# Eight norms of a two-block kernel: sums of squares with tokens on partitions, and one product that spreads the inverse

## The reference

```python
def layer_norm(x, g, b):                      # ln_in, and ln1 and ln2 of both layers
    mu = mean(x, -1); var = mean((x - mu)**2, -1)
    return (x - mu) * rsqrt(var + 1e-5) * g + b

def rms_norm(x, g):                           # before the mixer, before the experts, at the end
    return x * rsqrt(mean(x * x, -1) + eps) * g

x = layer_norm(x, ln_in)
for l in range(2):
    x = layer_norm(ALPHA * x + mixers(x), ln1[l])
    x = layer_norm(ALPHA * x + ffn(x), ln2[l])
x = x + g1 * mixer(modulate(rms_norm(x, norm1), ...))
x = x + g2 * experts(modulate(rms_norm(x, norm2), ...))
return rms_norm(x, final_norm)
```

## Time and profile before

| what | value |
|---|---|
| median of 3 executions | 3438.56 us (3436.9 to 3443.4) |
| profiled execution, its own time | 3444.45 us |
| span of its instructions | 3442.6 us |
| mean granted TensorE clock (of 1.00) | 0.976 |
| PE busy | 3278.4 us (95%) |
| DVE busy | 2461.8 us (72%) |
| ACT busy | 1684.0 us (49%) |

### The profile page before, as it was taken

One profiled execution on the slowest core, in us unless ns is written; L12 is line 12 of the kernel. 1 busy time (PEld: TensorE's weight loads), 2 busy tenths in 40 slices (PEclk: granted clock), 3 DMA queues, 4 the chain that ended last, 5 costly groups with the idle time before them and its releaser, 6 DMA issues.

```text
span 3442.6 us, 43580 instructions
## 1 busy us (share of the span) xinstructions
PE 3278.4 (95%) x13510; PEld 2317.1 (67%) x13510; DVE 2461.8 (72%) x2995; ACT 1684.0 (49%) x2237; POOL 484.7 (14%) x625
## 2 busy tenths in 40 slices
PE   8989999999988999979999999799999999999997
PEld 3453677774453777756646657688878887878885
DVE  4874655454954746554548984799999999999996
ACT  3332433232341423232221133588888888878884
POOL 0000000000000000000000000233434433343340
PEclk9989999999989999999999999899999999999999
DMA  5111334331101443321110022699999999999995
GB/s 199 61 31 43 115 118 135 117 92 61 50 25 49 132 138 116 117 98 43 50 61 13 25 80 86 213 354 367 371 354 358 373 372 351 366 365 357 361 375 194
DMA packets 168015, 618.37 MB, mean 180 GB/s; under 512 B 18528, under 2 KB 18656, under 8 KB 167328
## 3 DMA queue, kind: packets, MB, share of 16 engines
q1 hardware_dynamic: 157232, 573.90, 46.3%
q0 software_dynamic: 10672, 43.00, 4.4%
HBM read 587.99 MB, written 28.84 MB: 179 GB/s over the span
## 4 chain that ended last, share of the span: by engine, by line
PE 79%; DVE 13%; issue 3%; ACT 2%; DMA 2%; POOL 0%; DVEq 0%; ACTq 0%; POOLq 0%; SPq 0%
PE bank L605 52%; PE bank L1241 24%; DVE w_part L2665 2%; DMA sb_ring<-in_w 2%; DVE sb_work L1925 1%; DVE sb_rstd L1887 1%; PE bank L1231 1%; PE bank L1192 1%; PE bank L1249 1%; DVE sb_work L2073 0%; DVE sb_work L2431 0%; DVE sb_work L2387 0%; DVE sb_work L2698 0%; ACT w_part L1790 0%; DVE sb_work L2693 0%
## 5 line engine op out<-in xcount | busy, mean ns | idle before, releaser
L2665 DVE TENSOR_TENSOR w_part<-sb_ring,w_part 128x1024 fp32r<-128x1024 f32 x762 | 889.8, 1225 | 65.0 <-ACT w_part L1790 64.3
L1790 ACT ACTIVATE w_part<-sb_ring 128x1024 fp32r<-128x1024 f32 x762 | 770.0, 1053 | 82.4 <-PE bank L1241 53.8
L1241 PE MATMUL bank<-w_part,xg_hi 128*128 128x512 f32 x2048 | 564.0, 397 | 0.0
L605 PE MATMUL bank<-h_hi,split_part 128*128 128x512 f32 x1408 | 444.4, 400 | 7.9 <-ACT h_hi L1521 7.9
L1241 PEld LDWEIGHTS bank<-w_part,xg_hi 128*128 128x128 f32 x2048 | 383.0, 188 | 89.1
L1241 PE MATMUL bank<-w_part,xg_lo 128*128 128x512 f32 x1024 | 321.0, 395 | 0.0
L605 PEld LDWEIGHTS bank<-h_hi,split_part 128*128 128x128 f32 x1408 | 265.7, 190 | 80.4 <-issue 15.6
L1241 PE MATMUL bank<-w_part,act_hi 128*128 128x512 f32 x1024 | 284.9, 400 | 2.0 <-DVE act_lo L2708 0.9
L605 PE MATMUL bank<-sb_hT,sb_ring 128*128 128x512 f32 x576 | 261.6, 612 | 11.7 <-ACT sb_hT L1342 11.7
L605 PE MATMUL bank<-h_lo,split_part 128*128 128x512 f32 x704 | 272.3, 394 | 0.0
L605 PE MATMUL bank<-act_hi_ff,split_part 128*128 128x512 f32 x704 | 229.1, 407 | 5.7 <-DVE act_lo_ff L2246 5.7
(11 more groups left out here) (364 smaller groups left out, 4728.5 us busy)
## 6 DMA issues: line engine op xcount, KB each, us to landing
sb_ring<-in_w SPq DMA_DIRECT2D x768, 512.0 KB, 7.9
sb_ring<-in_wstream SPq DMA_DIRECT2D x304, 512.0 KB, 3.6
y_rows<-sb_padc POOLq DMA_DIRECT2D x1, 4096.0 KB, 17.7
sb_xT<-in_x SPq DMA_DIRECT2D x4, 512.0 KB, 7.2
x_rows<-sb_padc SPq DMA_DIRECT2D x1, 2048.0 KB, 9.8
residual<-sb_hT POOLq DMA_DIRECT2D x1, 2048.0 KB, 6.5
sb_hT<-residual POOLq DMA_DIRECT2D x1, 2048.0 KB, 8.1
x_rows<-sb_work SPq DMA_DIRECT2D x1, 2048.0 KB, 6.6
```

The source lines that it names most:

```text
L605: ins = nc.tensor.matmul(out, l, r, start=start, stop=stop)
L1241: ins = nc.tensor.matmul(out[n][:], l[:, k, :], r[:, n * 512:(n + 1) * 512], start=False, stop=(k, p) == (KD - 1, 2))
L1790: nc.scalar.activation(w_hi[t % SPLITS], ring[:, t % RING, :], ACT.Copy).then_inc(s_hi, 1)
L2665: nc.vector.tensor_tensor(w_lo[t % SPLITS], ring[:, t % RING, :], w_hi[t % SPLITS].bitcast(F32), ALU.subtract).then_inc(s_lo, 1)
```

## The change

Eight norms (`BY_TOKEN`, and ln1 and ln2 in both layers) get another way to their inverse. The tile `dev_tok` is new: 128 partitions x 2 slots x 8 columns.

- Sums: for each chunk k, and each of the four blocks b of 128 tokens, the 128x128 block of squares is now the stationary operand and two columns of `ones_d` are the moving one. 32 products of two columns take the place of 8 products of 512 columns. Tokens come out on partitions: 8 columns, two equal ones for each block.
- Root: on 8 columns, into `dev_tok`. Reciprocal: on the same 8 columns.
- New on VectorE: a multiplication of the identity (128x128, for all four blocks) by the inverse, broadcast along the free dimension, into `rstd`: four diagonal blocks side by side, 128x512.
- New on TensorE: one product of the 128x128 of ones with these 512 columns (`spread_inverse`), into a PSUM bank of its own. All partitions of it hold the inverse of all tokens.
- The scaling by gain and inverse reads the inverse from that bank.
- In `ln1` the modulation piece stands between the sums and the product that spreads.

```diff
+                if tag[0] in BY_TOKEN:
+                    state["var"] = bank("var", tag)
+                    for k in range(n):
+                        token_var(tag, k)
+                else:
+                    chunks(("var", tag), lambda k: ones, lambda k: squares(width)[:, at + k, :], n, width=width,
+                           ready=("square", tag))
                 if ("var", tag) in MOD_AT_SPOT:
                     modulation(MOD_AT_SPOT["var", tag])
+                if tag[0] in BY_TOKEN:
+                    spread_inverse(tag)
+
+            def token_var(tag, k):
+
+                pe.wait_ge(*reached("square", tag, k))
+                for b in range(TB):
+                    mm(state["var"][:, 2 * b:2 * b + 2], sq[:, k, b * P:(b + 1) * P], ones_d[:, 0:2], (k, b) == (0, 0), (k, b) == (KD - 1, TB - 1),
+                       *(("var", tag) if (k, b) == (KD - 1, TB - 1) else ()))
+
+            def spread_inverse(tag):
+
+                out = bank("inv", tag)
+                pe.wait_ge(dve_done, when("diag", tag))
+                mm(out[:], const("ones"), rstd[:, when("diag_slot", tag), :], True, True, "inv", tag)
...
+            state["var"] = bank("var", ("x1",))
             for k in range(KD):
-                running("var", ("x1",), sq, k, ("square", ("x1",)))
+                token_var(("x1",), k)
+            spread_inverse(("x1",))
...
                     if half == 1 and i in (4, 6, 8, 10):
-                        out2_var((i - 4) // 2)
+                        token_var(("x2",), (i - 4) // 2)
...
             for m in range(4, KD):
-                out2_var(m)
+                token_var(("x2",), m)
             state["job"] = 1
+            spread_inverse(("x2",))
...
                 if m >= 2:
-                    running("var", ("final",), sq, m - 2, ("square", ("final",)))
+                    token_var(("final",), m - 2)
...
+            spread_inverse(("final",))
...
+                if tag[0] in BY_TOKEN:
+                    slot = len(norms) % 2
+                    norms.append(tag)
+                    found[("diag_slot", tag)] = ("slot", slot)
+                    dev = dev_tok[:, slot, :]
+                    dve.wait_ge(act_done, when("deviation", tag))
+                    nc.vector.reciprocal(dev, dev).then_inc(dve_done, did.up())
+                    dve.wait_ge(dve_done, did.n)
+                    nc.vector.tensor_tensor(rstd[:, slot, :].rearrange("p (b t) -> p b t", t=P),
+                        const("ident").unsqueeze(1).to_broadcast([P, TB, P]), dev.rearrange("p (b n) -> p b n",
+                        n=2)[:, :, 0:1].to_broadcast([P, TB, P]), ALU.mult).then_inc(dve_done, did.up(("diag", tag)))
+                    dve.wait_ge(pe_done, when("full", "inv", tag))
+                    return bank_of("inv", tag)[:]
...
+BY_TOKEN = ("in", "ln1", "ln2", "x1", "x2", "final")
```

More of the change, by code:

```diff
@@ L292, in build @@
         probe = sb("probe", [P, 1])
+        dev_tok = sb("dev_tok", [P, 2, 2 * TB])
         b_t = sq[:, 0:GROUPS, :]
@@ L682, in norm @@
                     chunks(("mean", tag), lambda k: ones, lambda k: src[:, k, :], n)
-                chunks(("var", tag), lambda k: ones, lambda k: squares(width)[:, at + k, :], n, width=width,
-                       ready=("square", tag))
+                if tag[0] in BY_TOKEN:
[5 more added lines that the diff above has]
+                           ready=("square", tag))
                 if ("var", tag) in MOD_AT_SPOT:
                     modulation(MOD_AT_SPOT["var", tag])
+                if tag[0] in BY_TOKEN:
[9 more added lines that the diff above has]
+                mm(out[:], const("ones"), rstd[:, when("diag_slot", tag), :], True, True, "inv", tag)
             def running(kind, tag, src, k, ready):
@@ L1096, in yt @@
                 ins.then_inc(pe_done, did.up(("full", "yt", c)))
-            def out2_var(m):
-                pe.wait_ge(*reached("square", ("x2",), m))
-                mm(state["var"][:], ones_d, sq[:, m, :], m == 0, m == KD - 1, *((("var", ("x2",))) if m == KD - 1 else ()))
             def out2_products(half, outs, j, i):
@@ L1303, in _ @@
                        *(("sums", m) if b == TB - 1 else ()))
+                if m == 2:
+                    state["var"] = bank("var", ("final",))
                 if m >= 2:
-                    running("var", ("final",), sq, m - 2, ("square", ("final",)))
+                    token_var(("final",), m - 2)
             for k in (KD - 2, KD - 1):
-                running("var", ("final",), sq, k, ("square", ("final",)))
+                token_var(("final",), k)
+            spread_inverse(("final",))
         @block.scalar
@@ L1320, in deviation @@
                         act.wait_ge(dve_done, when("normed_all", norms[-2]))
-                    out = rstd[:, len(norms) % 2, 0:width]
+                    out = dev_tok[:, len(norms) % 2, :] if tag[0] in BY_TOKEN else rstd[:, len(norms) % 2, 0:width]
                     norms.append(tag)
+                if tag[0] in BY_TOKEN:
+                    width = 2 * TB
                 nc.scalar.activation(probe[0:1, :], const("ones")[0:1, 0:1], ACT.Sqrt).then_inc(act_done, did.up())
@@ L1904, in scaled @@
                         op0=ALU.mult, op1=ALU.mult).then_inc(dve_done, did.up(("normed", tag, k), *([("normed_all",
-                        tag)] if k == n - 1 else [])))
+                        tag), ("free", "inv", tag)] if k == n - 1 else [])))
             def rms_scaled(tag, dst, src, gain, width=T):
@@ L1911, in rms_scaled @@
                         op0=ALU.mult, op1=ALU.mult).then_inc(dve_done, did.up(("normed", tag, k), *([("normed_all",
-                        tag)] if k == KD - 1 else [])))
+                        tag), ("free", "inv", tag)] if k == KD - 1 else [])))
             def conv(dst, padded, taps, w):
```

## The result

The changed kernel takes 3476.36 us (median of 4 executions, 3473.32 to 3481.34) against 3440.94 us for the kernel before (4 executions, 3436.9 to 3443.4). The ratio is 1.0102, with a 95% interval of 1.0084 to 1.0120: slower by 35 us. 3461.6 was forecast, with a range that ended at 3474; with its fourth execution the kernel before has 3440.94 instead of the 3438.56 that the forecast started from. The side was right, and so was the mechanism within the norms. What happens between the norms was not, and the time lies 2.4 us above the range.

What follows compares the result with a forecast made beforehand. The prediction took PE as the bound, busy 95% of the span. Layer norms 11.1 + 8.6, `x1` 4.3, `x2` -0.3 and `final` -0.7 gave +23 us on 3438.56: 3461.6 us, range 3440 to 3474.

Steps and rivals of the forecast that it cites:

- The record of a two-column product: In the new sums, each of 64 records would take 0.112 us at full clock and 0.213 at half.
- The clock falls within the sums: In `in`, `ln1` and `ln2`, clock falls 2.2 us into the sums, which take 11.6 us against 7.1: +4.5 a norm.
- Root to first scaling: In the norms' chain, 3.3 us at half clock or 2.4 at full, against 4.1: -0.8 or -1.7.
- ln1: Spreading product waits behind modulation, +1.8; sums +4.5; feed-forward stage gets full clock sooner, -2.0: +4.3 us each, 8.6.
- x1: Sums wholly at half clock, 13.6 + 0.3 us against 8.8, +5.1; chain -0.8: +4.3 us.
- final: Root waits for ScalarE's table load and probe, not the sums; only the chain counts, at half clock: -0.7 us.
- x2: Only the last four chunks stand behind the long products; with the chain's -0.8, -0.3 us in all.
- Between the norms: Stages behind the norms: 0 for cold starts as now, and -2.0 us behind each `ln1`; -4.0 in all.
- Rival 1: Dense short products keep the clock full in the sums; total -17 us, 3422 us; 17 in 100.
- Rival 2: Weight loads in the sums don't follow the clock, or it falls late; 3436 to 3442 us, no change; 8 in 100.
- Rival 3: Clock falls at once in all `in`, `ln1`, `ln2` sums, nothing comes back in `ln1`; 3472 to 3476 us; 13 in 100.
- The mean clock: Over the whole kernel, the mean granted clock would fall by 0.0075, from 0.976 to about 0.969.

Runs made afterwards that it cites:

- early: The changed kernel with the spreading product of `ln1` issued ahead of the modulation piece; no total given, `x2`'s first scaling 25.3 us late, not 39.4.
- wide: The changed kernel with 128 moving columns instead of two in each product of the sums; 3432.37 us, ratio 0.9974 against the kernel before.
- no_ln: The changed kernel with `ln1` and `ln2` of both layers as before; no total given, `x2`'s first scaling 8.4 us later than before.
- keeper: The changed kernel with one more product of 504 columns per chunk of the sums, into columns nobody reads; 3576.52 us.

## Why the prediction was right and wrong

- **The record of a two-column product**, 0.112 at full clock and 0.213 at half: right. `x1` has 64 at half clock in 13.8 us, 0.213 each and the tail; `early` has 32 at full clock in 3.63 us. `wide` has 0.112 with 128 columns, so what moves doesn't make the period.
- **The clock falls within the sums**: right, and it decides the case, since `wide` undoes it and ends below before. **When it falls** was mis-sized: "With 3.9 us from there to the fall, it comes 2.2 us into the stage". In both `ln1` it did (2.3 and 2.2 us in), but in `in` and the two `ln2` the fall came 0.7, 1.6 and 0.5 us in. The five stages took 13.3, 11.8, 12.4, 11.8 and 13.4, on average 12.5 against the 11.6 of the forecast. Together they added 26.9 us and not 22.5, 4.4 more. The 3.9 us were taken from gaps after stages behind which PE did nothing, and there were but two of them in the rows (3.5 and 4.5).
- **Root to first scaling**: 3.4 to 3.5 at half clock, forecast 3.3; 2.5 at full clock (`wide`), forecast 2.4. Right.
- **`ln1`**: the spreading product does wait behind the modulation, at 0.8 us over before and not 1.8. The modulation held it until 376.43, 3.4 us after the root's start and not 3.8, and the clock came back at 377.2, while it ran, so that it took 1.5 us and not 2.0. So each `ln1` added 5.4 us and not the 6.3 of the forecast, an error that hides a part of the others. But "should have its full clock some 4 us sooner; by half of that, -2" failed. PE waited for the scaling, began the feed-forward stage at 379.6, and the clock fell again at 380.6 and stayed low until 387.4 (stretches above), as long as before the change. The stretch from `ln1`'s first scaling to the sums of `ln2` became 0.6 and 0.7 us longer in the two layers, against the -2.0 each of the forecast.
- **`x1`** +4.4, forecast +4.3. **`final`** -0.6, forecast -0.7. **`x2`** +0.5, forecast -0.3.
- **Between the norms**: this is the step that failed most. The forecast had -4.0 there: the two -2 of `ln1`, and "The next stage starts cold now and then, for about the same time: 0". Measured are +7.8. Behind `in` 1.6 us came back, but 0.6 and 0.7 were added behind the two `ln1`, 2.7 between `ln2` of the first and `ln1` of the second layer, and 5.3 between `x1` and `x2`. The runs show the cause of the last: the stage behind `x1` has other stretches at half clock when its work starts at another moment. That such a price exists stands nowhere in the forecast.
- **The sum**: +23 forecast, +35.4 measured by the medians. To `x2` it was +23.7 against +39.4 in the traces. Of the 15.7 us between them 11.8 lie between the norms (-4.0 forecast, +7.8 measured), 4.4 in the sums of the layer norms, 0.8 in `x2`, 0.3 in the start, 0.4 in the other chains; the chains of `ln1` were 2.0 better than forecast.
- **Rival 1**, the clock holds, was not the case, and its time of 3422 was too good: `wide` realises it and takes 3432, since the stage behind each norm goes on starting at half clock. **Rival 2**, loads that don't follow the clock, is refuted by 0.213. **Rival 3** had nearly the right time (3472 to 3476), in part by luck: of its two reasons, the fall came nearly at once in two norms of five and not in all, and nothing came back in `ln1`; the rest came from between the norms, which it doesn't name.
- **The mean clock** was forecast at 0.969 and is 0.961. Worked out from the mean clocks and the spans, the changed kernel is at half clock for some 100 us more than the one before (an estimate); the forecast counted 52.

The range was cut too tight above: all its upper end held was an earlier fall; it held nothing for work further on that meets the clock at another moment.

## What to carry to other kernels

A sum over partitions made of short products is paid by the record with its weight load and not by what moves: at full clock 0.112 us here, with 2 moving columns as with 128. So let the moving side be as wide as it can be at no cost; here 128 columns kept the clock through the stage, where 2, 32 and 64 lost it, and that alone turned +35 us into -7. In a kernel bound by TensorE, price every edit of a few us with a margin for the clock further on: 1.4 us of delay cost 6.5 more in a part that it did not touch, and 8.6 us (`no_ln`) cost 0.4 there.

## What was not expected of the hardware

- The four half-clock stretches behind `x1` repeated within 0.3 us in two executions of the same program, and the pattern there changed with a shift of 1.4 us ahead of it. Elsewhere the two executions differed in three places.
- Alternating 504-column and two-column products, each about half of a chunk's time, stayed at 0.50 for 25 us (`keeper`), busy throughout. Why long products didn't bring the clock back there is open.
- A reciprocal of 8 columns takes 0.20 us and one of 512 takes 3.35; a root of 8 columns out of PSUM takes 0.27, where 4 columns of another function took 0.155.
- Open: why the experts' stage differs by up to 10 us between traces; and why 2.7 us were added between the first `ln2` and the second `ln1`. Two stretches there bear on it: one at 944 is 6.6 us long at 0.50 where before (at 930) it is 3.2, and in `no_ln`, which adds nothing there, it is 3.2 (at 934). That the moment of the start makes this difference too is likely, but was not tried.
